# Activation tiles of a decoder kernel stored with padded rows

## Chip, cores and metric

The kernel runs on one core of a Trainium2 chip. The metric is the device time of one execution in microseconds; less is better.

## The reference

A trunk of two decoder layers over 256 tokens of width 1024, all in float32. Each layer:

```python
h = rms_norm(x, mix_norm[l])
z = h @ w_in[l]                       # 1024 -> 5632: u, q, k, v, two gates
y_a = s5_branch(u, ...)               # diagonal state-space scan, GELU, GLU
y_b = diff_attention(q, k, v, lam)    # 8 heads, two maps each
m = sigmoid(g_ssm) * (y_a @ w_proj_ssm[l]) + sigmoid(g_attn) * (y_b @ w_proj_attn[l])
x = x + m @ w_out[l]
h = rms_norm(x, ffn_norm[l])
f = swiglu(h, wg, wu, wd)             # layer 0: dense, 1024 -> 2816 -> 1024
f = moe_swiglu(h, ...)                # layer 1: the best 2 of 8 experts, each such a SwiGLU
x = x + f
```

A last RMSNorm ends it. Nearly all arithmetic is in products with weight matrices, about 390 MB of them in float32.

## The kernel before

**Products in three parts.** TensorE reads float32 operands as `fp32r`, which keeps fewer bits, so every operand is split into a high and a low part, and a product is made of three: high x high, low x high, high x low (`mm3`, L1938 to L1940). In the profile `psum<-w_hi,hsT_hi` names the moving operand first (w_hi, 512 columns wide) and the stationary one second (hsT_hi, 128 columns, loaded by an LDWEIGHTS of its own on PEld). The weight load for the next product runs while the present one streams.

**The weight stream.** All weights come as slots of 128 x 2048 floats. SP loads a slot into a ring `w_raw` (L660), ACT copies it to `w_hi` (rounding it, `act_split`, L599), DVE writes the rest to `w_lo` (`dve_split`, L605), PE uses the two. Segments 0 to 2 (mixer, dense layer, mixer) use a ring of three w_hi/w_lo places, the expert rounds five (two more, `w_hi_more` and `w_lo_more`). `split_of` gives the place of a slot; where the slot is to be stationary (`stationary`: gate and up slots of the dense layer outside ring position 1) it begins LEAD = 48 floats, 192 bytes, later.

**The activations.** They are needed with the model dimension on the partitions, so they are transposed on PE, copied out of PSUM by ACT (high part) and completed by DVE (low part). Four pairs of tiles matter:
- `hT_hi`, `hT_lo`: [128, 8, 256], the normed rows of all tokens in eight chunks. Stationary (128 of the 256 columns) for the 512-wide products of both mixers, written at L1009, L1140, L1463 and L1655; moving (all 256 columns) where the weights are stationary: the S5 input and the gate and up products of the dense layer. These are the 256-wide products.
- `hsT_hi`, `hsT_lo`: [128, 8, 128], the rows of one expert round, stationary for its gate and up products; written at L1195 and L1829.
- `eactT_hi`, `eactT_lo`: [128, 2, 4, 128], the activations of an expert round, stationary for its down products; written at L1216 and L1871.
- `actT`, `yS`, `yB`: the same for the dense layer and for the two mixer branches.

In all of them a chunk is a multiple of 512 bytes long, and so is each slot's. Before `w_lo` and before the region that begins with `a_q` the layout is rounded up so that they have the residue modulo 512 of `a_hT`; `w_hi` follows `w_raw` directly and has it too, since all ahead of it is a multiple of 512 long.

**The order.** Segment 0 (layer 0 mixer) lasts to about 254 us, segment 1 (dense layer) to 470, segment 2 (layer 1 mixer) to 685, then come eight expert rounds of 33 slots (`pe_round`; gate and up slots, with the down slots of earlier blocks between them). A round has 22 gate and up slots with 12 products each and 11 down slots with 12 each, 396 long products, and beside them 22 transposes of the activations and 8 of the next round's rows. In the dense layer the slots run g0, u0, g1, u1, d0, g2, u2, d1, and so on.

Of the kernel before, what the change touches and what calls it, by code (L numbers as in the profile page):

```python
# [8 lines left out]
F32 = mybir.dt.float32  # L9
F32R = mybir.dt.float32r  # L10
# [7 lines left out]
P = 128  # L18
SEQ, D, DEPTH = 256, 1024, 2
NT = SEQ // P  # L20
KD = D // P
# [23 lines left out]
SEG = 33  # L45
NRAW, NW, AHEAD = 4, 3, 2
LEAD = 48
RAW_POS = [i % 4 if i < 24 else (i - 24) % 3 for i in range(SEG)]
RAW_USES = [RAW_POS.count(p) for p in range(NRAW)]
GROUP_BLOCK = 512  # L50
# [148 lines left out]
def trunk(nc, t):  # L199
    ctx = ExitStack()  # L200
    with ctx:
        here = [(nc.sbuf_base + 63) // 64 * 64]

        def at(name, shape, dt, addr):
            return nc.alloc_sbuf_tensor_at(name, list(shape), dt, offset=addr)
# [7 lines left out]
        def sb(name, shape, dt=F32):  # L213
            a = here[0]
            here[0] += size(shape, dt)
            return at(name, shape, dt, a)

        def room(nbytes):
            a = here[0]
            here[0] += nbytes  # L220
            return a
# [3 lines left out]


        x = sb("x_tok", [P, NT, D])
        a_hT = room(16384)
        hTh = at("hT_hi", [P, KD, SEQ], F32R, a_hT)
        hTl = at("hT_lo", [P, KD, SEQ], F32R, a_hT + 8192)  # L230
        raw = sb("w_raw", [P, NRAW, SLOT])
        wh = sb("w_hi", [P, NW * SLOT + LEAD], F32R)
        here[0] += (a_hT - here[0]) % 512
        wl = sb("w_lo", [P, NW * SLOT + LEAD], F32R)
        ident = sb("ident", [P, P])
# [46 lines left out]


        here[0] += (a_hT - here[0]) % 512
        a_q, a_k, a_v = room(8192), room(8192), room(8192)
        a_u, a_yh, a_yl = room(4096), room(4096), room(4096)
        a_tab = room(32768)
        a_rr = room(16384)
# [44 lines left out]
        sg = at("silu_g", [P, 2 * SEQ], F32, a_q + 2048)  # L333
        aTh = at("actT_hi", [P, 2, 2, SEQ], F32R, a_u)
        aTl = at("actT_lo", [P, 2, 2, SEQ], F32R, a_yh)
        hsh = at("hsT_hi", [P, KD, P], F32R, a_k)
        hsl = at("hsT_lo", [P, KD, P], F32R, a_k + 4096)
        moe_act = at("eact_tok", [P, 512], F32, a_q)
        moe_sg = at("esilu_g", [P, 512], F32, a_q + 2048)
        bTh = at("eactT_hi", [P, 2, 4, P], F32R, a_hT)  # L340
        bTl = at("eactT_lo", [P, 2, 4, P], F32R, a_hT + 4096)
        rawx = at("w_raw_more", [P, 1, SLOT], F32, a_tab + 8192)
        whx = [at("w_hi_more0", [P, 1, SLOT], F32R, a_rr), at("w_hi_more1", [P, 1, SLOT], F32R, a_tab + 16384)]
        wlx = [at("w_lo_more0", [P, 1, SLOT], F32R, a_rr + 8192), at("w_lo_more1", [P, 1, SLOT], F32R, a_tab + 24576)]
# [98 lines left out]
        def bank(b):  # L443
            return PS[:, b, :]
# [107 lines left out]
        def raw_of(seg, i):  # L552
            p = (RAW_POS if seg < 3 else ROUND_POS)[i]
            return raw[:, p, :] if p < NRAW else rawx[:, 0, :]

        def stationary(seg, i):

            if seg == 1:
                return i % NW != 1 and FFN_SLOTS[i][0] != "d"
            return False  # L560

        def split_of(seg, i):

            p = i % NW if seg < 3 else ROUND_POS[i]
            if p < NW:
                a = (p + 2) % NW * SLOT + (LEAD if stationary(seg, i) else 0)
                return wh[:, a:a + SLOT], wl[:, a:a + SLOT]
            return whx[p - NW][:, 0, :], wlx[p - NW][:, 0, :]

        def landed(seg, i, r=None):  # L570

            if seg < 3:
                p = RAW_POS[i]
                return s_raw[p], 16 * (seg * RAW_USES[p] + RAW_POS[:i + 1].count(p))
            p = ROUND_POS[i]
# [70 lines left out]
        def _(sp):  # L646
            stream = t["stream"]

            def load(seg, i, src, r=None, ahead=False):

                if seg < 3:
                    before = seg * SEG + before_in(RAW_POS, i)
                    if before >= 0:
                        sp.wait_ge(s_lo, before + 1)
                elif r is PROLOGUE:

                    sp.wait_ge(s_lo, 3 * SEG + before_in(RAW_POS, i) + 1)
                else:
# [602 lines left out]
        def _(dve):  # L1261
            own = Own(dve, s_dve)
            V = nc.vector
# [187 lines left out]
            def lo_of(dst, src, hi, scale, n, last=True):  # L1451

                i = V.scalar_tensor_tensor(dst, src, scale, hi.bitcast(F32), ALU.mult, ALU.subtract)
                if last:
                    i.then_inc(s_trf[n % 2], 1)
# [96 lines left out]
            for l in range(DEPTH):  # L1552
# [9 lines left out]
                for s in range(SEG):  # L1562
# [3 lines left out]
                    if 0 <= s - 17 < HEADS:  # L1566
                        h = s - 17
                        n = TR_AT[l, "o", h]
# [23 lines left out]
                    if 0 <= s - 18 < HEADS:  # L1592
                        h = s - 18
                        n = TR_AT[l, "oT", h]
# [5 lines left out]
                    if 0 <= s - 16 < HEADS:  # L1600
                        h = s - 16
                        n = TR_AT[l, "wT", h]
# [47 lines left out]
                    if s in (28, 30):  # L1650
                        for g in (s - 28, s - 27):
                            n = TR_AT[l, "mT", g]
                            thi[0] += 1
                            dve.wait_ge(s_thi, thi[0])
                            lo_of(hTl[:, 2 * g:2 * g + 2, :].rearrange("p k n -> p (k n)"), bank(4 + n % 2),  # L1655
                                  hTh[:, 2 * g:2 * g + 2, :].rearrange("p k n -> p (k n)"), 0.5, n)
                    if s in (25, 26, 27, 29):
                        out_block(l, {25: PS0, 26: PS0 + 1, 27: PA0, 29: PA0 + 1}[s])
                    if s in (27, 29):
# [23 lines left out]
                n = 2 * l + 1  # L1683
# [90 lines left out]
            n = TR_AT[1, "logits", 0]  # L1774
# [23 lines left out]
            n = TR_AT[1, "places", 0]  # L1798
# [27 lines left out]
            V.tensor_tensor(G[:, :, :], oh1[:, :, :], oh2[:, :, :], ALU.add).then_inc(s_gates, 1)  # L1826

            def hs_lo(g):
                V.tensor_tensor(hsl[:, 4 * g:4 * g + 4, :].rearrange("p k n -> p (k n)"), bank(2 + g),  # L1829
                                hsh[:, 4 * g:4 * g + 4, :].rearrange("p k n -> p (k n)").bitcast(F32),  # L1830
                                ALU.subtract).then_inc(s_hsf, 1)

            dve_split(dve, 3, 1, PROLOGUE)
# [24 lines left out]
            def dve_round(r, first, last=False):  # L1858

                his = [0]  # L1860

                def hi_taken(name):

                    his[0] += 1
                    assert [w for w in ROUND_TR if w[:2] != "ST"][his[0] - 1] == name
                    dve.wait_ge(s_thi, r * NB + (THI0 + his[0]))
                    return TR0 + ROUND_TR.index(name)

                def act_lo(j):
                    t, n = hi_taken(f"act{j}"), block_width(j)  # L1870
                    V.tensor_tensor(bTl[:, j % 2, 0:n // P].rearrange("p k n -> p (k n)"), bank(4 + t % 2)[:, 0:n],  # L1871
                                    bTh[:, j % 2, 0:n // P].rearrange("p k n -> p (k n)").bitcast(F32),
                                    ALU.subtract).then_inc(s_trf[t % 2], 1)

                for i in range(SEG):
                    if last and i == 5:
                        dve.wait_ge(s_idx, 1)
                        dve.wait_ge(s_yw, r * 16)
                        V.tensor_copy(rowi[:, :, :], rowf[:, :, :]).then_inc(s_idx, 1)
                    if last and i in (10, 20):  # L1880
                        add_rows(i // 10 - 1)
                    if last and i == SEG - 1:
                        for q in range(NT):
                            n = TR0 + LAST_TR.index(f"ST{q}")
                            dve.wait_ge(s_tr, r * R_TR + (n + 1))
                            V.tensor_copy(ST[:, q * P:(q + 1) * P], bank(4 + n % 2)[:, 0:P]).then_inc(s_trf[n % 2], 1)
                    if i in (29, 31):
                        act_lo(4 + (i - 29) // 2)
                    if i in (30, 31) and not last:
                        dve.wait_ge(s_hsh, r * 2 + (2 + i - 29))  # L1890
                        hs_lo(i - 30)
                    if not last or i + RAHEAD < SEG:
                        round_split(dve_split, dve, i, r)
                    if last and i == 4:
                        own.do(V.tensor_copy(gcol[:, :], gateR[:, :, bass.ds(r, 1)].rearrange("p t o -> p (t o)")))
                    if i in (7, 13, 19, 25):
                        act_lo((i - 7) // 6)
                    if last and i == SEG // 2:
                        own.do(V.tensor_copy(pcol[:, :], placeR[:, :, bass.ds(r, 1)].rearrange("p t o -> p (t o)")))
                        select_last()  # L1900
                    if i in LAST_UP[:5] or i == 28:
                        j = LAST_UP.index(i) if i in LAST_UP else 5
                        n = block_width(j)
                        dve.wait_ge(s_sg, r * NB + (GU0 + j + 1))
                        if j == 5:
                            dve.wait_ge(s_tr, r * R_TR + (TR0 + ROUND_TR.index("act4") + 1))
                        ups = bank(3 + 4 * (j % 2)) if j < NB - 1 else bank(2 + 4 * (j % 2))[:, n:2 * n]
                        V.tensor_tensor(moe_act[:, 0:n], moe_sg[:, 0:n], ups[:, 0:n], ALU.mult).then_inc(s_act, 1)

                for c in range(2 if last else 0):  # L1910
                    dve.wait_ge(s_ysh, r * 2 + (2 + c + 1))
                    V.tensor_tensor(ysl[:, c * 512:(c + 1) * 512], bank(c), ysh[:, c * 512:(c + 1) * 512].bitcast(F32),
                                    ALU.subtract).then_inc(s_ysl, 1)
# [577 lines left out]
```

## Time and profile before

| | us |
|---|---|
| median of 3 runs | 1453.68 |
| lowest, highest | 1452.29, 1455.04 |
| span of the profiled execution | 1453.1 |
| PE busy | 1426.3 (98%) |
| PEld busy (weight loads) | 1202.9 (83%) |
| DVE busy | 1179.7 (81%) |
| ACT busy | 884.7 (61%) |

The profile is one execution, taken by the hardware profiler. Its engines: PE for matmuls, PEld for weight loads, which overlap PE, DVE, ACT, POOL, and SP, which here issues loads. A matmul's record is longer than its place in the stream: neighbouring records overlap. What a matmul costs in a run of equal ones is therefore read from the starts of neighbours in the timeline, not from its duration. Starts are printed to 0.01 us; over n spacings the error of the mean is 0.01 us / n.

### The profile page before, as it was taken

What the parts mean: (1) busy time and instruction counts of PE and PEld (TensorE: products, weight loads), DVE (VectorE), ACT (ScalarE), POOL (GpSimd) and SP (SyncE); (2) the same over time, 40 slices, a digit from 0 to 9 for tenths busy, and PEclk for the clock granted to TensorE, in tenths of its full rate; (3) what the DMA queues carried; (4) which work ended last, traced back from release to release, by engine and by line L of the source; (5) the groups of instructions that cost most, each with busy time, mean ns of one, the idle gap of its engine ahead of it and who ended that gap; (6) DMA issues with size and microseconds to landing.
All of it is one profiled execution on the core that took longest, in us unless ns stands there. A gap on an engine that the chain in (4) does not pass through costs nothing.

```text
span 1453.1 us, 22261 instructions
## 1 busy us (share of the span) xinstructions
PE 1426.3 (98%) x8381; PEld 1202.9 (83%) x8381; DVE 1179.7 (81%) x1181; ACT 884.7 (61%) x879; POOL 141.4 (10%) x195
## 2 busy tenths in 40 slices
PE   8999999999999999999999999999999999999997
PEld 6887888999998888887888888888888888888875
DVE  7998886676467697876988988889898898898896
ACT  5334754534344345644768768777777777777774
POOL 1910100000000000101960000000000000000100
PEclk9999999999999999999999999999999999999999
DMA  7443445776455442454999999999999999999993
GB/s 285 136 180 121 156 159 189 261 246 233 151 189 192 174 160 97 151 188 161 365 413 390 406 363 399 380 364 413 353 398 394 354 404 370 379 397 347 419 376 145
DMA packets 94247, 408.87 MB, mean 281 GB/s; under 512 B 28769, under 2 KB 43233, under 8 KB 47714
## 3 DMA queue, kind: packets, MB, share of 16 engines
q1 hardware_dynamic: 75984, 391.37, 69.9%
q10 hardware_dynamic: 17042, 12.36, 2.6%
q0 software_dynamic: 1152, 4.19, 0.7%
q8 instruction: 46, 0.75, 0.2%
q14 instruction: 23, 0.19, 0.0%
HBM read 390.98 MB, written 14.16 MB: 279 GB/s over the span
## 4 chain that ended last, share of the span: by engine, by line
PE 78%; DVE 11%; DMA 3%; SPq 3%; issue 2%; ACT 2%; POOL 1%; DVEq 0%; POOLq 0%; ACTq 0%
PE psum L1938 25%; PE psum L1940 24%; PE psum L1939 24%; DVE w_lo L605 4%; SPq L696 3%; PE psum L1954 2%; DMA w_raw<-in_stream 2%; DMA x_normed<-y_rows,row_number 1%; ACT w_hi L599 1%; ACT square_out L993 0%; PE psum L2284 0%; PE psum L2005 0%; DVE s_r L1511 0%; ACT prob L1129 0%; PE psum L1987 0%
## 5 line engine op out<-in xcount | busy, mean ns | idle before, releaser
L605 DVE TENSOR_TENSOR w_lo<-w_raw,w_hi 128x2048 fp32r<-128x2048 f32 x267 | 607.9, 2293 | 130.2 <-ACT w_hi L599 129.4
L599 ACT ACTIVATE w_hi<-w_raw 128x2048 fp32r<-128x2048 f32 x267 | 509.4, 1915 | 251.1 <-PE psum L1940 191.5
L1938 PE MATMUL psum<-w_hi,hsT_hi 128*128 128x512 f32 x448 | 176.0, 393 | 0.8 <-DVE hsT_lo L1829 0.8
L1940 PE MATMUL psum<-w_lo,hsT_hi 128*128 128x512 f32 x448 | 174.5, 390 | 0.0
L1939 PE MATMUL psum<-w_hi,hsT_lo 128*128 128x512 f32 x448 | 174.3, 389 | 0.0
L1938 PE MATMUL psum<-w_hi,hT_hi 128*128 128x512 f32 x376 | 152.7, 406 | 1.8 <-ACT gate_ssm L1075 1.4
L605 DVE TENSOR_TENSOR w_lo_more<-w_raw,w_hi_more 128x2048 fp32r<-128x2048 f32 x56 | 128.2, 2289 | 24.3 <-ACT w_hi_more L599 23.6
L1940 PE MATMUL psum<-w_lo,hT_hi 128*128 128x512 f32 x376 | 147.4, 392 | 0.0
L1939 PE MATMUL psum<-w_hi,hT_lo 128*128 128x512 f32 x376 | 147.1, 391 | 0.0
L599 ACT ACTIVATE w_hi_more<-w_raw 128x2048 fp32r<-128x2048 f32 x56 | 107.1, 1913 | 21.6 <-DMA w_raw<-in_stream 12.4
L1938 PE MATMUL psum<-hT_hi,w_hi 128*128 128x256 f32 x416 | 116.6, 280 | 0.2 <-DVE hT_lo L1463 0.2
L1940 PE MATMUL psum<-hT_lo,w_hi 128*128 128x256 f32 x416 | 116.5, 280 | 0.0
L1939 PE MATMUL psum<-hT_hi,w_lo 128*128 128x256 f32 x416 | 116.3, 280 | 0.0
L1938 PE MATMUL psum<-w_hi_more,hsT_hi 128*128 128x512 f32 x256 | 101.2, 395 | 0.0
L1940 PE MATMUL psum<-w_lo_more,hsT_hi 128*128 128x512 f32 x256 | 99.8, 390 | 0.0
L1939 PE MATMUL psum<-w_hi_more,hsT_lo 128*128 128x512 f32 x256 | 99.6, 389 | 0.0
L1938 PEld LDWEIGHTS psum<-w_hi,hsT_hi 128*128 128x128 f32 x448 | 84.1, 188 | 17.8 <-DVE w_lo L605 1.0
L1940 PEld LDWEIGHTS psum<-w_lo,hsT_hi 128*128 128x128 f32 x448 | 84.1, 188 | 17.8
L1939 PEld LDWEIGHTS psum<-w_hi,hsT_lo 128*128 128x128 f32 x448 | 84.2, 188 | 17.0
L605 DVE TENSOR_TENSOR w_lo_more<-w_raw_more,w_hi_more 128x2048 fp32r<-128x2048 f32 x40 | 91.4, 2285 | 1.2 <-ACT w_hi_more L599 1.2
L1938 PE MATMUL psum<-w_hi,eactT_hi 128*128 128x512 f32 x224 | 89.7, 401 | 1.6 <-DVE eactT_lo L1871 1.6
L1940 PE MATMUL psum<-w_lo,eactT_hi 128*128 128x512 f32 x224 | 87.4, 390 | 0.0
(429 smaller groups left out, 2651.2 us busy)
## 6 DMA issues: line engine op xcount, KB each, us to landing
w_raw<-in_stream SPq DMA_DIRECT2D x323, 1024.0 KB, 6.9
w_raw_more<-in_stream SPq DMA_DIRECT2D x40, 1024.0 KB, 7.7
h_rows<-one_row ACTq DMA_DIRECT2D x10, 512.0 KB, 6.6
round_rows<-h_rows SPq DMA_DIRECT2D x7, 512.0 KB, 7.0
y_rows<-y_slots ACTq DMA_DIRECT2D x7, 512.0 KB, 9.2
y_rows<-one_row ACTq DMA_DIRECT2D x4, 512.0 KB, 6.2
gain_row<-in_gain_rows SPq DMA_DIRECT2D x3, 512.0 KB
x_tok<-in_x SPq DMA_DIRECT2D x2, 512.0 KB, 6.2
```

The lines of the kernel that those rows point to most:

```text
L599: nc.scalar.activation(split_of(seg, i)[0], raw_of(seg, i), ACT.Copy).then_inc(s_hi, 1)
L605: nc.vector.tensor_tensor(l_, raw_of(seg, i), h.bitcast(F32), ALU.subtract).then_inc(s_lo, 1)
L696: sp.dma_start(zT[rows(g, q), j, :, :], quad(U4, g, j, q)).then_inc(s_zt, 16)
L1938: mm(out, lh, rh, start=start, stop=False)
L1939: mm(out, ll, rh, start=False, stop=False)
L1940: return mm(out, lh, rl, start=False, stop=stop)
L1954: i = nc.tensor.transpose(dst[:, k * P:(k + 1) * P], s, ident[:, :])
```

## The change

The rows of three pairs of tiles get a few floats of padding: 4 floats behind each 256 of hT, 16 behind each 128 of hsT, 20 behind each 128 of eactT. The rows of hT are then 1040 bytes apart, those of hsT 576, those of eactT 592. Every use reads and writes the unpadded part. Three DVE writers that treated several rows as one flat row now use them as rows. hsT grows by 1024 bytes, so what lies behind `a_k` moves by 1024 bytes; hT grows by 256 bytes in all, which moves `w_raw` and `w_hi` by 256, and the rounding ahead of `w_lo` takes these up. No instruction is added or taken away.

```diff
+HT_PAD, HS_PAD, BT_PAD = 4, 16, 20
...
-        a_hT = room(16384)
-        hTh = at("hT_hi", [P, KD, SEQ], F32R, a_hT)
-        hTl = at("hT_lo", [P, KD, SEQ], F32R, a_hT + 8192)
+        hT_bytes = 4 * KD * (SEQ + HT_PAD)
+        a_hT = room(2 * hT_bytes)
+        hTh = at("hT_hi", [P, KD, SEQ + HT_PAD], F32R, a_hT)[:, :, 0:SEQ]
+        hTl = at("hT_lo", [P, KD, SEQ + HT_PAD], F32R, a_hT + hT_bytes)[:, :, 0:SEQ]
         raw = sb("w_raw", [P, NRAW, SLOT])
         wh = sb("w_hi", [P, NW * SLOT + LEAD], F32R)
         here[0] += (a_hT - here[0]) % 512
...
-        a_q, a_k, a_v = room(8192), room(8192), room(8192)
+        hs_bytes = 4 * KD * (P + HS_PAD)
+        a_q, a_k, a_v = room(8192), room(2 * hs_bytes), room(8192)
...
-        hsh = at("hsT_hi", [P, KD, P], F32R, a_k)
-        hsl = at("hsT_lo", [P, KD, P], F32R, a_k + 4096)
+        hsh = at("hsT_hi", [P, KD, P + HS_PAD], F32R, a_k)[:, :, 0:P]
+        hsl = at("hsT_lo", [P, KD, P + HS_PAD], F32R, a_k + hs_bytes)[:, :, 0:P]
...
-        bTh = at("eactT_hi", [P, 2, 4, P], F32R, a_hT)
-        bTl = at("eactT_lo", [P, 2, 4, P], F32R, a_hT + 4096)
+        bT_bytes = 4 * 8 * (P + BT_PAD)
+        bTh = at("eactT_hi", [P, 2, 4, P + BT_PAD], F32R, a_hT)[:, :, :, 0:P]
+        bTl = at("eactT_lo", [P, 2, 4, P + BT_PAD], F32R, a_hT + bT_bytes)[:, :, :, 0:P]
...
-                V.tensor_tensor(hsl[:, 4 * g:4 * g + 4, :].rearrange("p k n -> p (k n)"), bank(2 + g),
-                                hsh[:, 4 * g:4 * g + 4, :].rearrange("p k n -> p (k n)").bitcast(F32),
+                V.tensor_tensor(hsl[:, 4 * g:4 * g + 4, :], bank(2 + g).rearrange("p (k n) -> p k n", n=P),
+                                hsh[:, 4 * g:4 * g + 4, :].bitcast(F32),
                                 ALU.subtract).then_inc(s_hsf, 1)
```

The low parts of hT at L1655 and of eactT at L1871 change in the same way as that of hsT.

## Rows read from the trace of the kernel before

**Rows 1.** The page: busy time, slices, loads, the chain that ended last.

```profile
PE 1426.3 (98%) x8381; PEld 1202.9 (83%) x8381; DVE 1179.7 (81%) x1181; ACT 884.7 (61%) x879; POOL 141.4 (10%) x195
PEclk9999999999999999999999999999999999999999
GB/s 285 136 180 121 156 159 189 261 246 233 151 189 192 174 160 97 151 188 161 365 413 390 406 363 399 380 364 413 353 398 394 354 404 370 379 397 347 419 376 145
PE 78%; DVE 11%; DMA 3%; SPq 3%; issue 2%; ACT 2%; POOL 1%; DVEq 0%; POOLq 0%; ACTq 0%
PE psum L1938 25%; PE psum L1940 24%; PE psum L1939 24%; DVE w_lo L605 4%; SPq L696 3%; PE psum L1954 2%; DMA w_raw<-in_stream 2%; DMA x_normed<-y_rows,row_number 1%; ACT w_hi L599 1%; ACT square_out L993 0%; PE psum L2284 0%; PE psum L2005 0%; DVE s_r L1511 0%; ACT prob L1129 0%; PE psum L1987 0%
```

**Rows 2.** Timeline of PE in a round: start, duration, line; first and last of 22.

```profile
800.03 0.39 PE L1940 MATMUL psum<-w_lo,hsT_hi 128*128 128x512 f32 x1
...
804.79 0.39 PE L1940 MATMUL psum<-w_lo,hsT_hi 128*128 128x512 f32 x1
```

**Rows 3.** The same in the dense layer: ends of slots u0, g1 with u1, g2 with u2.

```profile
260.45 0.28 PE L1938 MATMUL psum<-hT_hi,w_hi 128*128 128x256 f32 x1
...
266.21 0.28 PE L1938 MATMUL psum<-hT_hi,w_hi 128*128 128x256 f32 x1
...
277.09 0.40 PE L1938 MATMUL psum<-w_hi,actT_hi 128*128 128x512 f32 x1
...
282.55 0.28 PE L1938 MATMUL psum<-hT_hi,w_hi 128*128 128x256 f32 x1
...
293.86 0.40 PE L1938 MATMUL psum<-w_hi,actT_hi 128*128 128x512 f32 x1
```

**Rows 4.** Timeline: bf16 fillers; and their group, with the mean of one.

```profile
249.36 2.85 PE L1960 MATMUL psum<-maskb,identb 128*128 128x128 bf16 x48
...
L1960 PE MATMUL psum<-maskb,identb 128*128 128x128 bf16 x176 | 11.3, 219 | 0.0
```

**Rows 5.** Groups by line, one of three lines each: busy us, mean ns, idle before.

```profile
L1938 PE MATMUL psum<-w_hi,hsT_hi 128*128 128x512 f32 x448 | 176.0, 393 | 0.8 <-DVE hsT_lo L1829 0.8
L1938 PE MATMUL psum<-w_hi,hT_hi 128*128 128x512 f32 x376 | 152.7, 406 | 1.8 <-ACT gate_ssm L1075 1.4 <-DVE hT_lo L1463 0.4
L1938 PE MATMUL psum<-hT_hi,w_hi 128*128 128x256 f32 x416 | 116.6, 280 | 0.2 <-DVE hT_lo L1463 0.2
L1938 PE MATMUL psum<-w_hi_more,hsT_hi 128*128 128x512 f32 x256 | 101.2, 395 | 0.0
L1938 PE MATMUL psum<-w_hi,eactT_hi 128*128 128x512 f32 x224 | 89.7, 401 | 1.6 <-DVE eactT_lo L1871 1.6
L1938 PE MATMUL psum<-w_hi_more,eactT_hi 128*128 128x512 f32 x128 | 49.9, 390 | 0.0
```

**Rows 6.** The writers, by line: ns minimum/median/maximum, first and last start.

```profile
L1463 DVE TENSOR_TENSOR hT_lo<-psum,hT_hi x16: 672/682/692, 15.0 to 682.2; 128x512 fp32r<-128x512 f32 x16
L1829 DVE TENSOR_TENSOR hsT_lo<-psum,hsT_hi x16: 680/684/692, 691.7 to 1342.1; 128x512 fp32r<-128x512 f32 x16
L1009 ACT ACTIVATE hT_hi<-psum x16: 576/594/603, 12.7 to 681.6; 128x512 fp32r<-128x512 f32 x16
L1195 ACT ACTIVATE hsT_hi<-psum x16: 597/600/602, 690.0 to 1340.5; 128x512 fp32r<-128x512 f32 x16
```

**Rows 7.** Timeline of PE after an interruption in a round.

```profile
805.02 0.60 PE L1954 MATMUL psum<-ident,eact_tok 128*128 128x128 f32 x4
805.38 0.48 PE L1938 MATMUL psum<-w_hi,hsT_hi 128*128 128x512 f32 x1
805.69 0.40 PE L1939 MATMUL psum<-w_hi,hsT_lo 128*128 128x512 f32 x1
...
807.55 0.39 PE L1938 MATMUL psum<-w_hi,hsT_hi 128*128 128x512 f32 x1
```

**Rows 8.** Stretches: busy us (x instructions) of each engine, clock, DMA share, GB/s.

```profile
800.00:893.30 93.30, 93.30 (x427) 77.28 (x426) 82.25 (x48) 70.53 (x50) 0.00 (x0) 1.00 0.96 383
893.30:986.60 93.30, 93.30 (x427) 77.29 (x426) 82.03 (x48) 69.36 (x49) 0.00 (x0) 1.00 0.96 383
...
0.00:130.00 130.00, 123.38 (x1047) 101.67 (x1049) 118.82 (x210) 55.68 (x61) 47.93 (x58) 0.99 0.53 192
```

**Rows 9.** Waits from 700 to 1340 us: total us, times, longest.

```profile
DVE w_lo L605 <- ACT w_hi L599: 36.6, 63, 1.2
ACT w_hi L599 <- DMA w_raw<-in_stream: 33.2, 39, 2.0
```

**Rows 10.** The chain that ended last, its longest pieces: start, us, what.

```profile
59.79 1.57 DVE setup_tmp L1437
...
1345.42 9.52 DMA w_raw<-in_stream
...
1365.67 11.95 DMA x_normed<-y_rows,row_number
...
1391.31 10.05 DMA w_raw<-in_stream
```

**Rows 11.** Waits of SP's queue: total us, times, longest.

```profile
SPq L660 <- DVE w_lo L605: 876.0, 244, 21.8
```

More of the change, by code:

```diff
@@ L1654, in _ @@
                             dve.wait_ge(s_thi, thi[0])
-                            lo_of(hTl[:, 2 * g:2 * g + 2, :].rearrange("p k n -> p (k n)"), bank(4 + n % 2),
-                                  hTh[:, 2 * g:2 * g + 2, :].rearrange("p k n -> p (k n)"), 0.5, n)
+                            lo_of(hTl[:, 2 * g:2 * g + 2, :], bank(4 + n % 2).rearrange("p (k n) -> p k n", k=2),
+                                  hTh[:, 2 * g:2 * g + 2, :], 0.5, n)
                     if s in (25, 26, 27, 29):
@@ L1870, in act_lo @@
                     t, n = hi_taken(f"act{j}"), block_width(j)
-                    V.tensor_tensor(bTl[:, j % 2, 0:n // P].rearrange("p k n -> p (k n)"), bank(4 + t % 2)[:, 0:n],
-                                    bTh[:, j % 2, 0:n // P].rearrange("p k n -> p (k n)").bitcast(F32),
+                    V.tensor_tensor(bTl[:, j % 2, 0:n // P], bank(4 + t % 2)[:, 0:n].rearrange("p (k n) -> p k n", n=P),
+                                    bTh[:, j % 2, 0:n // P].bitcast(F32),
                                     ALU.subtract).then_inc(s_trf[t % 2], 1)
```

## The prediction

> **What bounds the kernel now.** I read the page first: PE is busy 98% of the span, its clock is 9 tenths or more in every slice, and the chain that ended last is PE for 78%, 73% of the span on the three product lines L1938 to L1940 [rows 1]. A busy PE is not yet a paced PE, because the matmul records overlap (390 ns each), so I went on to the starts of neighbouring matmuls. In the expert rounds (columns 512 wide, slots w_hi and w_lo moving, hsT stationary) 22 starts lie between 800.03 and 804.79 us with nothing else among them: 4.76 us / 21 = 226.7 ns from one to the next [rows 2]. That is the real price of a product.
>
> How much of it is streaming? Two shapes tell. The same products 256 wide, in the dense layer's second slot, take (266.21 - 260.45) / 48 = 120.0 ns [rows 3]. The 256 further columns cost 106.7 ns, so a column takes 0.417 ns (the 2.4 GHz level) and 512 columns 213.3 ns. So **13.3 ns** of every long product is no streaming, and 13.3 ns of the short ones too. The bf16 fillers, 128 wide, show how small that remainder can be: 47 spacings in 2.85 - 0.22 = 2.63 us are 56.0 ns each, 53.3 of it streaming, so 2.7 ns [rows 4].
>
> Is that remainder a matter of addresses? In the dense layer it is. Slots there are stationary, and `stationary()` starts them 192 bytes late (LEAD), except those in ring position 1. The second slot, without LEAD, gives 120.0 ns; the next two, with LEAD, give (277.09 - 266.21) / 96 = 113.3 ns; the pair before the second down slot, also with LEAD, gives (293.86 - 282.55) / 96 = 117.8 ns [rows 3]. Same shape, same engines, same clock: 192 bytes between the residues of the two operands are worth 2.2 ns or 6.7 ns. They are two steady values for one layout, so the state in which a run of products is entered counts as well. All other operands meet at equal residues, and all their long runs settle at 226 to 227 ns.
>
> The Trainium skill speaks against this change. SBUF — State Buffer, section Who interferes with whom, gives TensorE two independent read ports and says that PE never waits on anyone; by that the residues would change nothing. The 113.3 against 120.0 ns above is hard to reconcile with it. The sum below goes by the rows.
>
> **The change, part by part.**
>
> *Residues.* Rows of hT are now 1040 bytes, so its eight chunks begin at 0, 16, ... 112 modulo 512 (hT_lo 128 further); hsT steps by 64 through all of 0 to 448; eactT steps by 80, also eight values. Counts of products that read them as stationary, 512 wide: hsT 3 x (448 + 256) = 2112, eactT 3 x (224 + 128) = 1056, hT 3 x 376 = 1128 and 24 in the first slot [rows 5]. hT as moving operand: 3 x 416 = 1248.
>
> *The slot ring.* A side effect: the two hT tiles grow from 16384 to 16640 bytes, and w_hi lies behind w_raw with no alignment of its own, so the whole w_hi ring moves by 256 modulo 512. w_lo is aligned and stays. Two of three long products move w_hi, so yS, yB and actT, which nobody padded, meet it 256 bytes apart as well (552 long products); w_hi_more stays where it was.
>
> *Writers.* ACT and DVE now write rows with gaps. The trace has both forms. DVE takes 682 ns for 128x512 into four separate rows (L1463) and 684 ns into one flat row (L1829); ACT takes 594 against 600 ns (L1009, L1195) [rows 6]. Nothing, and none of them stands in the path for long. I take 0.
>
> *What a long product then costs* is not in this trace: no long product with unequal residues settles in it. Bounds from the nearest rows. Below: the best short product with unequal residues, 6.7 ns less. Still lower, the bf16 remainder of 2.7 ns in place of 13.3, 10.6 ns less. Above: the spacing before a run has settled. After the four transposes at 805.02 the starts from 805.69 to 807.55 are eight spacings of 232.5 ns, **5.8 ns more** than settled [rows 7]. For hsT and eactT, which go through eight residues, I take the middle of the two measured gains, (2.2 + 6.7) / 2 = 4.4 ns. For hT, whose shift stays small, I take 2.2 ns. For the 1248 short products, which have most of their offset already, 0 (bounds -4.5 and +2.2 ns from 117.8, so -5.6 to +2.7 us), and 0 for the 552 unpadded ones (-3.7 to +3.2 us).
>
> *What of it reaches the end.* The rounds run at a fixed period: 427 matmuls in each 93.3 us, PE never without work [rows 8]. From 700 to 1340 us no wait of PE is in the list, and those of ACT and DVE are covered [rows 9]. So a gain there counts in full, as long as the stream of weights follows. The last round is different: its chain has waits for w_raw loads (9.52 and 10.05 us), for the gather of y_rows (11.95 us) and for issue [rows 10]. And the first 130 us have the DVE, busy 118.8 of 130 us [rows 8], with chains of w_lo, setup and s_r pieces [rows 10]; the q, k, v and gate products of layer 0 lie there. I count seven rounds of eight, 7 x 396 = 2772 products (of 3168), and of the 1152 long hT products the 660 outside those 130 us.
>
> *The weights.* A round moves 383 GB/s with a DMA share of 0.96 to 0.97; the queue waits for w_lo to free a slot, and one slice reached 413, another 419 GB/s [rows 1, 8, 11]. At 413 a round could not be shorter than 93.3 x 383 / 413 = 86.5 us. A gain of 4.4 ns x 396 = 1.7 us leaves 91.6 us, at 390 GB/s: it fits. ACT already waits 33.2 us in these rounds for loads [rows 9], so a much larger gain would be cut short here, while the slots hold.
>
> **The sum:** 2772 x 4.4 ns = 12.2 us, 660 x 2.2 ns = 1.5 us, together 13.7 us. The profiled span is 1453.1 us, which is 0.6 us under the median of the three times, 1453.68, and inside their range; I take the 13.7 us off the median: **1440 us**.
>
> **Rivals.**
>
> *A. The settled state is lost* (slower). After an interruption the spacings wander (between 220 and 240 ns by the starts) and then stop at 226.7, and stay there for as long as each product is followed by an equal one [rows 7]. With padded rows no product is: the residue changes with every k, and w_hi and w_lo now differ by 256. If settling needs a constant pattern, every long product keeps the unsettled mean, 5.8 ns more. Price: (2772 + 660) x 5.8 = 19.9 us, and the 552 unpadded add up to 3.2: 1474 to 1477 us; half of it, when only some residues are bad, 1464 us. For it speaks that unsettled spacings are nearly all above the settled one. Against it, that three unequal-residue pairs of slots are faster, and steady. It decides from the point where the mean of long products passes 226.7 ns.
>
> *B. The remainder goes nearly whole* (much faster). Each long product falls towards 216.0 ns: (2772 + 660) x 10.6 = 36.4 us, 1417 us. A round would be 89.1 us, at 401 GB/s; the loads would just follow. For it, only the bf16 row, whose weights are smaller.
> In a sentence of its own: TensorE: Matmul & The Clock Gate, section Back-to-back issue gap, gives an isolated gap of N / 2.4 + 2.5 ns, that is an estimate of about 216 ns for 512 columns; by the skill that would be the price already today, and the trace's 226.7 does not agree.
>
> *C. Nothing for long products.* The relief belongs to short ones, where the load of the next weights (188 ns a record) fills the whole product, and a long one has 100 ns left after it. Or the independent ports of the skill hold after all, and the differences in rows 3 have another cause. Time 1453 us, plus or minus 2.
>
> *D. A smaller gain*: only 2.2 ns on everything, 3432 x 2.2 = 7.6 us, 1446 us.
>
> **How the numbers follow.** Forecast (4.4 ns, own range 1432 to 1443) 0.33; D (1444 to 1450) 0.14; B (below 1432) 0.10; C 0.15; A 0.28, of it 0.18 below 1468 and 0.10 above. About 0.2% (2.9 us) is what a measurement can tell from no change. Faster: 0.33 + 0.14 + 0.10 = 0.57; same 0.15; slower 0.28. The range for 8 in 10 leaves out the outer part of B and of A: 1420 to 1468 us. It crosses zero because no row shows a long product with unequal residues; without A it would be 1432 to 1450.
>
> **What would show it.** In the profile after: counts of instructions as before; spacing of long hsT products near 222 ns, and rounds of about 91.6 us, for the forecast; 232 ns and over 95 us for A; 226.7 ns for C. The ratio of w_raw slots (w_hi shifted) to w_raw_more slots (w_hi_more not shifted) shows what the ring's 256 bytes do. DVE and ACT writers should stay at 684 and 600 ns. The prediction is wrong if the spacing falls and the rounds stay at 93.3 us (then the loads were the bound), or if the clock or another engine has changed.

## The result, and the profile after

The change makes the kernel slower: 1470.93 us median (1467.13 to 1471.58, 4 runs) against 1452.99 us (1451.63 to 1455.04, 4 runs) for the kernel before in the same comparison. The ratio is 1.012, 95% interval 1.0105 to 1.0134. The forecast was 1440 us: the sign was wrong, and the time lies 2.9 us above the range.

The page of the profile after, its busy line, clock line and chain. All lines of the code stand 4 lower than before, so the products are L1942 to L1944:

```profile
span 1469.0 us, 22261 instructions
PE 1442.8 (98%) x8381; PEld 1204.2 (82%) x8381; DVE 1180.3 (80%) x1181; ACT 882.9 (60%) x879; POOL 141.5 (10%) x195
PEclk9999999999999999999999999999999999999999
PE 87%; DVE 8%; ACT 1%; SPq 1%; issue 1%; DMA 1%; POOL 0%; POOLq 0%; DVEq 0%; ACTq 0%
PE psum L1942 27%; PE psum L1943 27%; PE psum L1944 27%; PE psum L1958 3%; DVE w_lo L609 3%; SPq L700 1%; DMA w_raw<-in_stream 1%; PE psum L2009 1%; ACT square_out L997 0%; PE psum L2054 0%; PE psum L2288 0%; ACT w_hi L603 0%; ACT prob L1133 0%; PE psum L2070 0%; PE psum L1991 0%
```

The same instructions (8381 matmuls, as in [rows 1]), the same clock, the other engines busy for the same time within 2 us. PE is busy 16.5 us longer, and the span is 15.9 us longer than the 1453.1 before. The chain is PE for 87% instead of 78% [rows 1]: PE covers what it had waited for.

Where it went is told by the windows (busy us and number of instructions of PE, PEld, DVE, ACT and POOL, then clock, DMA share, GB/s):

```profile
800.00:895.10 95.10, 95.10 (x427) 77.45 (x426) 81.65 (x48) 70.56 (x50) 0.00 (x0) 1.00 0.96 375
895.10:990.20 95.10, 95.10 (x428) 77.45 (x427) 82.13 (x49) 70.02 (x50) 0.00 (x0) 1.00 0.95 375
0.00:130.00 130.00, 122.22 (x1037) 99.67 (x1039) 118.38 (x210) 55.66 (x61) 47.94 (x58) 1.00 0.55 192
```

A round's 427 matmuls take 95.10 us where they took 93.3 [rows 8]. The stream of weights now moves 375 GB/s instead of 383. It is slower because PE is, not the reverse: ACT waits less for loads in the rounds than before, 25.6 us over 640 us of rounds (715 to 1355 us) against the 33.2 of [rows 9]. The 1.8 us are 4.5 ns for each of the 396 long products. The spacing itself is read from starts in the timeline of PE:

```profile
800.02 0.40 PE L1942 MATMUL psum<-w_hi_more,hsT_hi 128*128 128x512 f32 x1
...
804.88 0.39 PE L1942 MATMUL psum<-w_hi_more,hsT_hi 128*128 128x512 f32 x1
...
886.77 0.39 PE L1942 MATMUL psum<-w_hi,hsT_hi 128*128 128x512 f32 x1
...
906.00 0.40 PE L1944 MATMUL psum<-w_lo,hsT_hi 128*128 128x512 f32 x1
```

The first two are 21 spacings: 4.86 / 21 = 231.4 ns; the last two are 83, over seven slots, five of them with w_hi and two with w_hi_more: 19.23 / 83 = **231.7 ns**, against 226.7 [rows 2]. Slots with w_hi_more, whose place in memory did not move by 256, and slots with w_hi, which did, cost the same: taken apart over the whole trace, the mean is 231.7 ns for either. Two more pairs from the same timeline, the unpadded yB (its w_hi is 256 bytes off) and the short products of g2 and u2:

```profile
208.51 0.39 PE L1942 MATMUL psum<-w_hi,yB_hi 128*128 128x512 f32 x1
...
219.17 0.39 PE L1944 MATMUL psum<-w_lo,yB_hi 128*128 128x512 f32 x1
...
283.91 0.28 PE L1942 MATMUL psum<-hT_hi,w_hi 128*128 128x256 f32 x1
...
295.30 0.40 PE L1942 MATMUL psum<-w_hi,actT_hi 128*128 128x512 f32 x1
```

10.66 / 47 = 226.8 ns for yB, unchanged. 11.39 / 96 = 118.6 ns for the short ones, 0.8 more than the 117.8 of [rows 3]. The writers, with rows that have gaps (ns minimum, median, maximum; first and last start):

```profile
L1199 ACT ACTIVATE hsT_hi<-psum x16: 597/599/600, 694.0 to 1356.8; 128x512 fp32r<-128x512 f32 x16
L1833 DVE TENSOR_TENSOR hsT_lo<-psum,hsT_hi x16: 678/682/692, 695.7 to 1358.4; 128x512 fp32r<-128x512 f32 x16
```

599 and 682 ns against 600 and 684 [rows 6]: nothing.

Last, marks by which the two traces can be laid side by side: fillers at the ends of the first mixer, of the dense layer and of the second mixer, the transposes of eact_tok, those of round_rows. Four lines of before (the first fillers of before stand in [rows 4]), then the five of after:

```profile
450.98 0.40 PE L1960 MATMUL psum<-maskb,identb 128*128 128x128 bf16 x4
676.88 2.17 PE L1960 MATMUL psum<-maskb,identb 128*128 128x128 bf16 x36
L1954 PE MATMUL psum<-ident,eact_tok x176: 270/272/273, 711.7 to 1434.9; 128*128 128x128 f32 x176
L2284 PE MATMUL psum<-ident,round_rows x56: 270/272/273, 776.7 to 1340.2; 128*128 128x128 f32 x56
```

```profile
250.26 2.85 PE L1964 MATMUL psum<-maskb,identb 128*128 128x128 bf16 x48
453.17 0.40 PE L1964 MATMUL psum<-maskb,identb 128*128 128x128 bf16 x4
680.83 2.17 PE L1964 MATMUL psum<-maskb,identb 128*128 128x128 bf16 x36
L1958 PE MATMUL psum<-ident,eact_tok x176: 270/273/273, 716.1 to 1450.7; 128*128 128x128 f32 x176
L2288 PE MATMUL psum<-ident,round_rows x56: 271/273/273, 782.2 to 1356.5; 128*128 128x128 f32 x56
```

The first fillers (249.36 before) are 0.9 us late, the first eact_tok 4.4, the first round_rows 5.5, the last round_rows 16.3, the last eact_tok 15.8, the end 15.9. So the loss grows by 10.8 us over the six rounds between 777 and 1340 us, and the last round does not grow at all. The marks ahead of the rounds are less sure. The one at 451 us stands at 449.2 in a run in which nothing ahead of the rounds was padded (e2 below), so 2 us there are no price. The second mixer by itself, from the second fillers to the third, is steadier: 225.9 us before, 227.7 after, 225.9 in e2. Its 576 long hT products cost 1.8 us, 3.1 ns each.

### The profile page after: what moved, and what is told of

Its sections match the earlier page's. It is cut to its first block, busy times and chain, and to the rows that moved or that the text cites. A ratio compares the mean times of both kernels' runs of the same rounds, so it can differ in the third digit from the quotient of the medians.

```text
span 1469.0 us, 22261 instructions
## 1 busy us (share of the span) xinstructions
PE 1442.8 (98%) x8381; PEld 1204.2 (82%) x8381; DVE 1180.3 (80%) x1181; ACT 882.9 (60%) x879; POOL 141.5 (10%) x195
## 4 chain that ended last, share of the span: by engine, by line
PE 87%; DVE 8%; ACT 1%; SPq 1%; issue 1%; DMA 1%; POOL 0%; POOLq 0%; DVEq 0%; ACTq 0%
PE psum L1942 27%; PE psum L1943 27%; PE psum L1944 27%; PE psum L1958 3%; DVE w_lo L609 3%; SPq L700 1%; DMA w_raw<-in_stream 1%; PE psum L2009 1%; ACT square_out L997 0%; PE psum L2054 0%; PE psum L2288 0%; ACT w_hi L603 0%; ACT prob L1133 0%; PE psum L2070 0%; PE psum L1991 0%
## 5 line engine op out<-in xcount | busy, mean ns | idle before, releaser
L1942 PE MATMUL psum<-w_hi,hsT_hi 128*128 128x512 f32 x448 | 178.1, 397 | 0.8 <-DVE hsT_lo L1833 0.8
L1944 PE MATMUL psum<-w_lo,hsT_hi 128*128 128x512 f32 x448 | 176.3, 394 | 0.0
L1942 PE MATMUL psum<-w_hi,hT_hi 128*128 128x512 f32 x376 | 153.1, 407 | 2.0 <-ACT gate_ssm L1079 1.4
L1944 PE MATMUL psum<-w_lo,hT_hi 128*128 128x512 f32 x376 | 148.5, 395 | 0.0
L1942 PE MATMUL psum<-hT_hi,w_hi 128*128 128x256 f32 x416 | 117.3, 282 | 0.7 <-DVE w_lo L609 0.5
L1944 PE MATMUL psum<-hT_lo,w_hi 128*128 128x256 f32 x416 | 116.8, 281 | 0.0
L1942 PE MATMUL psum<-w_hi_more,hsT_hi 128*128 128x512 f32 x256 | 102.3, 400 | 0.0
L1944 PE MATMUL psum<-w_lo_more,hsT_hi 128*128 128x512 f32 x256 | 100.8, 394 | 0.0
L1942 PEld LDWEIGHTS psum<-w_hi,hsT_hi 128*128 128x128 f32 x448 | 84.4, 188 | 19.7 <-DVE w_lo L609 0.9
L1944 PEld LDWEIGHTS psum<-w_lo,hsT_hi 128*128 128x128 f32 x448 | 84.2, 188 | 19.7
L1942 PE MATMUL psum<-w_hi,eactT_hi 128*128 128x512 f32 x224 | 90.2, 402 | 0.0
L1943 PE MATMUL psum<-w_hi,eactT_lo 128*128 128x512 f32 x224 | 88.6, 395 | 0.0
```

The source lines that it names most:

```text
L1942: mm(out, lh, rh, start=start, stop=False)
L1943: mm(out, ll, rh, start=False, stop=False)
L1944: return mm(out, lh, rl, start=False, stop=stop)
```

## The experiments

Every kernel below is the kernel before with the edit shown (and with the three DVE writers in their form by rows); the ratio is to the kernel before on the same chip. "Distance" is the start of the stationary operand less that of the moving one, modulo 512 bytes. Before, it is 0 for all long products; for the short ones it is 192, and 0 in ring position 1 of the dense layer and in the S5 input. The spacings are means over settled runs of equal products, in which nothing else stands.

### e1_ring_64: only the moving operand's place

```diff
+        room(64)
         wh = sb("w_hi", [P, NW * SLOT + LEAD], F32R)
```

No tile is padded; the three w_hi places lie 64 bytes later, w_hi_more stays.

> Only the w_hi ring moves, by 64 bytes; all stationary tiles stay unpadded and w_lo and w_hi_more stay where they were. Theory T (a run of products settles when the stationary chunks keep one residue; where the moving operand begins does not matter): w_hi products stay at 226.7 ns, the time within 0.2% of before. Rival R (the residue between moving and stationary operand sets the spacing, and 256 bytes happened to be as good as 0): products with w_hi moving leave 226.7 ns, those with w_hi_more do not; at 5 ns on two thirds of some 3400 products on the path that is 11 us, about 1464 us.

Measured: 1468.94 us, ratio 1.0101 (1.0082 to 1.0119). A w_hi slot and the w_hi_more slot behind it, in the timeline:

```profile
889.62 0.39 PE L1941 MATMUL psum<-w_lo,hsT_hi 128*128 128x512 f32 x1
...
894.52 0.39 PE L1941 MATMUL psum<-w_lo,hsT_hi 128*128 128x512 f32 x1
...
895.20 0.39 PE L1941 MATMUL psum<-w_lo_more,hsT_hi 128*128 128x512 f32 x1
...
899.96 0.39 PE L1941 MATMUL psum<-w_lo_more,hsT_hi 128*128 128x512 f32 x1
```

4.90 / 21 = 233.3 ns, and three products later 4.76 / 21 = 226.7 ns. The same stationary tile, the same clock, the same shape: 64 bytes in the start of one operand make 6.6 ns. Theory T is refuted and rival R holds, with a higher price than the 5 ns that it was given. It holds for all stationary tiles: hsT 233.4, hT 232.5, actT 233.4, yB 233.3, yS 233.6. The Trainium skill, SBUF — State Buffer, section Who interferes with whom, lets PE's two ports work independently and never wait; this pair of slots disagrees with what one would conclude from it, that the starts of operands are indifferent. Only the two w_hi products of a chunk stand 64 bytes away, yet the mean over all three is 233.3. Which of the three steps is the long one is no fixed matter: for hsT the steps behind the two w_hi products are 234.8 and 234.3 ns and the one behind the w_lo product (its distance is 0) 231.5; for actT they are 230.9, 233.4 and 236.2.

### e2, e3, e4: one pair of tiles at a time

```diff
# e2_hsT_only
+        hsh = at("hsT_hi", [P, KD, 144], F32R, a_k + 0)[:, :, 0:P]
# e3_eactT_only
+        bTh = at("eactT_hi", [P, 2, 4, 148], F32R, a_hT + 0)[:, :, :, 0:P]
# e4_hT_only
+        hTh = at("hT_hi", [P, KD, 260], F32R, a_hT + 0)[:, :, 0:SEQ]
```

The low tiles change in the same way, and what lies behind a tile moves by a multiple of 512 bytes. e4 also brings the 256 bytes of the w_hi ring. The spacings in the expectations are those of the profile after; what is tested is the time of each part and whether the other tiles stay.

> Only hsT is padded (16 floats). hsT products 231.6 ns instead of 226.7, eactT and hT products stay at 226.7 ns. 2112 products, about 1848 of them in the seven rounds that PE sets: 4.9 ns x 1848 = 9 us, about 1462 us. If the padded tiles act only together, no change.

> Only eactT is padded (20 floats). eactT products 232.1 ns, the others stay: 924 products in seven rounds x 5.4 ns = 5 us, about 1458 us.

> Only hT is padded (4 floats), and with it the w_hi ring moves by 256 bytes as in the change. Long hT products 231.5 ns, short ones 118.7 instead of 118.1, hsT and eactT stay at 226.7 ns: 660 x 4.8 + 1000 x 0.6 = 4 us, about 1457 us. If it was the ring's 256 bytes that cost, the hsT products with w_hi slow down here too and those with w_hi_more do not, and the time comes near 1465 us.

| | median us | ratio (95%) | more us | spacing of the padded tile |
|---|---|---|---|---|
| hsT only | 1462.33 | 1.0062 (1.0043 to 1.0081) | 9.0 | 231.5 |
| eactT only | 1458.72 | 1.0032 (1.0019 to 1.0046) | 4.7 | 232.1 |
| hT only | 1455.39 | 1.0021 (1.0009 to 1.0032) | 3.0 | 231.6 |

The extra microseconds are (ratio - 1) x 1453. All other tiles stay at 226.7 ns in each of the three, in e4 with w_hi 256 bytes away as well, so the ring's 256 bytes are free. The parts add up to 16.7 us, against 17.4 for the whole change (0.012 x 1453): no interplay is needed. Each part is also its count times its spacing: hsT 2112 x 7/8 x 4.8 ns = 8.9 us; eactT 1056 x 7/8 x 5.4 ns = 5.0 us; hT 660 x 4.9 ns = 3.2 us. The last of the three agrees by luck. The 660 is the prediction's count, and the trace of before has 816 long hT products behind 130 us; 576 of them, the second mixer, cost 3.1 ns each (above), not 4.9. A likely reason, not tested: before the change many of them stand in stretches of twelve between interruptions, and those take 228 to 231 ns already.

### e5, e6: a constant distance, no padding

Is the loss due to the change of residue from product to product, as rival A had it, or to the distance as such? Here whole tiles begin later, so the distance is the same in every product of a run.

```diff
# e5_const_a: hT 64, hsT 128, eactT 192 bytes later
+        hTh = at("hT_hi", [P, KD, 256], F32R, a_hT + 64)[:, :, 0:SEQ]
+        hsh = at("hsT_hi", [P, KD, 128], F32R, a_k + 128)[:, :, 0:P]
+        bTh = at("eactT_hi", [P, 2, 4, 128], F32R, a_hT + 192)[:, :, :, 0:P]
# e6_const_b: hT 192, hsT 64, eactT 128
```

The low tiles move with the high ones here and in e9 to e11.

> No padding. Whole tiles begin later by a constant: hT by 64 bytes, hsT by 128, eactT by 192 (high and low parts alike). Theory E (a long product is cheap only where stationary and moving operand begin at equal residues modulo 256): all three leave 226.7 ns, hT for about 233, hsT and eactT for something between 227 and 236; the time rises by 10 to 20 us. Rival K (what matters is that the distance between the operands stays the same from product to product): all three settle, at 226.7 ns or at a value of their own below it, and the time stays at 1453 us or falls.

> As the run before with other constants: hT 192, hsT 64, eactT 128 bytes; in the dense layer hT then meets the gate and up slots at distance 0 instead of 192, except the second slot. E: long products 228 to 236 ns, each offset the same in either tile, and short gate and up products at 120.0 ns (the second slot's 117.8 or 113.3). K: long products settled at 226.7 ns or lower.

Measured: e5 1470.95 us, ratio 1.0119 (1.0102 to 1.0136); e6 1470.87 us, 1.0124 (1.0107 to 1.0141). In the timeline of e5, 46 spacings with hT at distance 64:

```profile
235.06 0.39 PE L1939 MATMUL psum<-w_hi,hT_lo 128*128 128x512 f32 x1
...
245.79 0.40 PE L1940 MATMUL psum<-w_lo,hT_hi 128*128 128x512 f32 x1
```

In that of e6, the same 46 with hT at distance 192, the 96 short products of g2 and u2, now at distance 0, and 83 spacings with hsT at 64:

```profile
234.95 0.39 PE L1939 MATMUL psum<-w_hi,hT_lo 128*128 128x512 f32 x1
...
245.49 0.40 PE L1940 MATMUL psum<-w_lo,hT_hi 128*128 128x512 f32 x1
...
283.85 0.28 PE L1938 MATMUL psum<-hT_hi,w_hi 128*128 128x256 f32 x1
...
295.36 0.39 PE L1938 MATMUL psum<-w_hi,actT_hi 128*128 128x512 f32 x1
...
884.22 0.40 PE L1938 MATMUL psum<-w_hi,hsT_hi 128*128 128x512 f32 x1
...
903.58 0.40 PE L1940 MATMUL psum<-w_lo,hsT_hi 128*128 128x512 f32 x1
```

10.73 / 46 = 233.3 ns at distance 64, 10.54 / 46 = 229.1 ns at 192, 19.36 / 83 = 233.3 ns at 64 again. Constant distances settle too, only at another value: theory E holds, rival K does not. What settles is the mean. Single steps go in a fixed pattern, 235.8 and 230.8 ns in turn for hsT at 64, where at distance 0 every step is 226 or 227. And the short products went from 117.8 to 11.51 / 96 = 119.9 ns by being brought to distance 0. **Distance 0 is the best of these for long products and the worst for short ones.** That is the pair of facts on which the prediction broke.

### e8 to e11: the table of distances

A kernel e7, with hT at 256, hsT at 32 and eactT at 16 bytes, gave no result. The distances 16 and 32 were measured in e9 and e11 in its place, and 256 with hsT.

```diff
# e8_steps: eactT steps by 768 bytes (distances 0 and 256 in turn), hsT by 544 (32-byte steps)
+        bTh = at("eactT_hi", [P, 2, 4, 192], F32R, a_hT + 0)[:, :, :, 0:P]
+        hsh = at("hsT_hi", [P, KD, 136], F32R, a_k + 0)[:, :, 0:P]
# e9_const_d: hsT 32, eactT 96 bytes later, short products at 64
+LEAD = 16
+        hsh = at("hsT_hi", [P, KD, 128], F32R, a_k + 32)[:, :, 0:P]
+        bTh = at("eactT_hi", [P, 2, 4, 128], F32R, a_hT + 96)[:, :, :, 0:P]
# e10_const_e: hsT 160, eactT 224, LEAD = 56 (short ones at 224)
# e11_const_f: hsT 256, eactT 16, LEAD = 32 (short ones at 128)
```

> Rows padded: eactT by 64 floats (chunks begin at 0 and 256 in turn), hsT by 8 floats (32 bytes a step). E: eactT stays at 226.7 ns although its residue modulo 512 changes with every chunk; hsT rises as in the change, to 229 to 232 ns, 4 to 9 us. If any change of the residue is what costs, eactT rises to 232 ns too.

> Constants again, no padding: hsT 32 bytes, eactT 96; hT stays, but the gate and up slots of the dense layer begin 64 bytes late instead of 192 (LEAD = 16). Theory E: 0 and 256 are the only good distances, so hsT lies between 227 and 233 ns and eactT between 230 and 234. A rival says that only multiples of 64 bytes matter: then hsT stays at 226.7. The short products at distance 64: one of the two settled values 113.3 or 117.8 ns; if 113.3 everywhere, the dense layer gains 1008 x 4.5 = 4.5 us.

> hsT 160 bytes, eactT 224, LEAD = 56 (224 bytes). E with a smooth dependence on the distance: hsT near 231 ns, eactT near 228. Short products at distance 224 between 113.3 and 120 ns.

> hsT 256 bytes, eactT 16, LEAD = 32 (128 bytes). E: hsT stays at 226.7 ns although it lies 256 bytes off; eactT near 227 to 230. Short products at distance 128: 119 to 120 ns, as hT at that distance in an earlier run.

| | median us | ratio (95%) |
|---|---|---|
| e8_steps | 1461.91 | 1.0063 (1.0047 to 1.008) |
| e9_const_d | 1471.34 | 1.0118 (1.0088 to 1.0147) |
| e10_const_e | 1469.71 | 1.0106 (1.0073 to 1.0139) |
| e11_const_f | 1456.30 | 1.0026 (1.0013 to 1.0039) |

Timeline of e8: 22 spacings of eactT; then 83 of hsT.

```profile
1157.09 0.39 PE L1939 MATMUL psum<-w_hi,eactT_lo 128*128 128x512 f32 x1
...
1162.08 0.39 PE L1940 MATMUL psum<-w_lo_more,eactT_hi 128*128 128x512 f32 x1
```

```profile
878.67 0.39 PE L1938 MATMUL psum<-w_hi,hsT_hi 128*128 128x512 f32 x1
...
897.87 0.39 PE L1940 MATMUL psum<-w_lo,hsT_hi 128*128 128x512 f32 x1
```

4.99 / 22 = 226.8 ns for eactT: chunks at changing places, 0 and 256, cost nothing there. In the whole trace they are not quite free: of the 81 stretches of eactT 24 take 229.8 to 230.2 ns, a value that no stretch of before has. That is some 0.8 us (an estimate, a quarter of 924 products at 3.1 ns). 19.20 / 83 = 231.3 ns for hsT: steps of 32 bytes cost as much as steps of 64. Timeline of e9, hsT at 32; of e11, hsT at 256 and eactT at 16, in two stretches:

```profile
882.88 0.40 PE L1938 MATMUL psum<-w_hi,hsT_hi 128*128 128x512 f32 x1
...
902.25 0.39 PE L1940 MATMUL psum<-w_lo,hsT_hi 128*128 128x512 f32 x1
```

```profile
879.12 0.40 PE L1938 MATMUL psum<-w_hi,hsT_hi 128*128 128x512 f32 x1
...
897.95 0.40 PE L1940 MATMUL psum<-w_lo,hsT_hi 128*128 128x512 f32 x1
...
780.38 0.39 PE L1939 MATMUL psum<-w_hi,eactT_lo 128*128 128x512 f32 x1
...
785.37 0.39 PE L1940 MATMUL psum<-w_lo_more,eactT_hi 128*128 128x512 f32 x1
...
1247.78 0.40 PE L1939 MATMUL psum<-w_hi,eactT_lo 128*128 128x512 f32 x1
...
1252.91 0.40 PE L1940 MATMUL psum<-w_lo_more,eactT_hi 128*128 128x512 f32 x1
```

19.37 / 83 = 233.4 ns at 32, 18.83 / 83 = 226.9 at 256. At 16 bytes the first stretch takes 4.99 / 22 = 226.8 ns and the second, of the same products in a later round, 5.13 / 22 = 233.2; 62 of the 81 stretches of eactT are at 226.7. The expectation of e10 failed: it had 231 ns at 160 and 228 at 224, and both took 233.3 or a little more. In e9 hsT left 226.7 at 32 bytes, so not only multiples of 64 cost. Of the two values for the short products nearly all took the dearer, 117.8. All constant distances together (ns from one product to the next; two values: both occur as settled states; a range: stretches of the trace differ, and most lie in it):

| distance | 0 | 16 | 32 | 64 | 96 | 128 | 160 | 192 | 224 | 256 |
|---|---|---|---|---|---|---|---|---|---|---|
| long, 512 wide | 226.7 | 226.7 / 233.3 | 233.4 | 233.3 | 234.3 | 231.7 to 233.3 | 233.3 to 233.8 | 228.9 to 229.5 | 233.3 | 226.7 to 226.9 |
| short, 256 wide | 120.0 | | | 113.3 / 117.8 | | 118.7 / 120.0 | | 113.3 / 117.8 | 116.7 / 117.8 | |

So 256 is as good as 0, and 16 bytes can be enough for the whole price. That the other distances repeat after 256 bytes too (320 like 64, say) was not run by itself. For long products nothing tried is better than what the kernel before has. For short ones 224 bytes (116.7) might be a little better than the 192 it has; by 1.1 ns on the some 1000 short products outside ring position 1 that would be 1 us, under what can be measured here, and it was not run by itself.

### e12_low_only: which step grows

```diff
+        hTl = at("hT_lo", [P, KD, 256], F32R, a_hT + 8384)[:, :, 0:SEQ]
+        hsl = at("hsT_lo", [P, KD, 128], F32R, a_k + 4160)[:, :, 0:P]
+        bTl = at("eactT_lo", [P, 2, 4, 128], F32R, a_hT + 4224)[:, :, :, 0:P]
```

Only the low tiles lie later (hT_lo 192, hsT_lo 64, eactT_lo 128), so one product in three has a distance.

> Only the low stationary tiles move, by a constant: hsT_lo 64 bytes, eactT_lo 128, hT_lo 192; high tiles at 0. Three products per chunk: (w_hi moving, high stationary), (w_hi, low), (w_lo, high); the weights of each are loaded while the one before it streams. Theory C (the load of the next weights collides with the stream that runs meanwhile): the step that grows most is the one behind the product during which the low tile is loaded, (w_hi, hsT_hi), to about 234 ns, the other two less, to 229 to 232. Rival W (a product waits for its own weights, so the low one starts late, or is slow itself): the step behind (w_hi, hsT_lo) grows most. Mean of hsT products between 229 and 233 ns, time 1460 to 1470 us; if one disturbed load in three were all that counts, the mean would be 226.7 + 6.6 / 3 = 228.9 ns and the time 1457 us.

Measured: 1466.09 us, ratio 1.009 (1.006 to 1.0119). Timeline:

```profile
802.66 0.39 PE L1938 MATMUL psum<-w_hi,hsT_hi 128*128 128x512 f32 x1
802.89 0.40 PE L1939 MATMUL psum<-w_hi,hsT_lo 128*128 128x512 f32 x1
803.13 0.39 PE L1940 MATMUL psum<-w_lo,hsT_hi 128*128 128x512 f32 x1
803.35 0.39 PE L1938 MATMUL psum<-w_hi,hsT_hi 128*128 128x512 f32 x1
```

For hsT the step behind L1939, the product whose own two operands differ, is the longest: 235.8 ns in the mean over the seven-slot stretches; behind L1940 it is 228.3, behind L1938 229.2. Rival W said this, and the 234 ns behind L1938 that theory C expected did not come. Yet it does not decide between them, since single steps do not show whose operands cost:

- In the same run the steps of eactT stand in another order, 234.4 behind L1938, 232.7 behind L1939 and 230.9 behind L1940.
- Where all three products have the same distance the steps differ as much: 230.9, 231.7 and 237.4 for hsT at 160 (e10).
- In e2 the steps in chunks whose distance is 0 are 235.7, 228.3 and 229.1, where a product that is charged its own distance would take 226.7.

What e12 does show is the mean. It is 231.1 ns, all three steps are above 226.7, and a mean of the table would be (2 x 226.7 + 233.3) / 3 = 228.9. So in a mixed pattern a product is not simply charged its own distance. Whether the load of the next weights takes part stays open.

## Why the prediction was wrong, step by step

**The bound: right.** PE at a fixed period sets the time. The spacing changed, and rounds went from 93.3 to 95.10 us while PE stayed busy throughout. The terms that were set to zero were zero: DVE and ACT writers (682 and 599 ns), the unpadded tiles (226.8), the 256 bytes of the ring (231.7 with w_hi_more and with w_hi; 226.7 for hsT with either in e4). The products in the first 130 us indeed count for little: +0.9 us in all by the fillers at 250 us. The count behind them was wrong, though: 816 long hT products start after 130 us, not 660. It hardly moved the sum (156 x 2.2 ns = 0.3 us). Seven rounds of eight indeed: between the last round_rows and the last eact_tok lie 94.7 us before and 94.2 after, though its products are slower too, and 94.9 and 94.8 in e9 and e10, where they are slower still. What covers them is read from the chain: the 11.95 us for y_rows and the two loads of 9.52 and 10.05 us stand in the chain of before [rows 10], the chain after has no such pieces, and its page has DMA at 1% instead of 3%. That link was read from the two chains and not tested by a run.

**The step that failed** is the one that begins "For hsT and eactT, which go through eight residues, I take the middle of the two measured gains". The gains (2.2 and 6.7 ns, [rows 3]) were measured on 256-wide products with w_hi as the stationary operand, and were carried over to 512-wide ones. The measured value is +4.9 ns, not -4.4. Same bytes, same engine, opposite sign: e6 shows both in one kernel, 119.9 ns for short products at distance 0 and 229 to 233 ns for long ones away from it. The reasoning before it, that 13.3 ns of either shape are "no streaming" and so one and the same remainder, could not have come out otherwise: a price per column that is taken from the difference of two widths leaves the same remainder in both. Where both stand 64 bytes apart the same sum gives (233.3 - 117.8) / 256 = 0.451 ns a column and 2.3 ns left, so it is no term that the two shapes share. And 226.7 and 120.0 are the best of the long and the worst of the short ones. Even for short products 4.4 ns was too much: of the 21 slots with LEAD in the trace of before 19 take 117.8 ns (2.2 less), and only g1 and u1 take 113.3. The step for hT (2.2 ns less) failed in the same way (231.6, 4.9 more), and the short products took 0.8 ns more where 0 stood, within its bounds.

**Rival A had the sign and nearly the size.** Both of its signs came, a spacing near 232 ns (231.7) and rounds of over 95 us (95.10). It took 5.8 ns from the unsettled spacings [rows 7], 19.9 us; measured are 4.9 ns and 17.4 us. Its count of 3432 products x 4.9 ns gives 16.8 us. Its mechanism is right in part at most. Constant distances settle in the mean, at 233.3 ns (e5, e6), and changing ones at 226.8 when they are multiples of 256 (e8): most of the loss is the distance itself. That the mixed patterns of e1 and e12 cost more than the mean of the table, and that a quarter of the stretches in e8 take 3 ns more, leaves room for something of A. For the whole change the table gives, for the four distances of hsT modulo 256, (226.7 + 233.3 + 233.3 + 229.2) / 4 = 230.6 ns; measured 231.7.

**Rival C's evidence was there and got too little weight.** It said that the relief belongs to short products. It expected 226.7 for long ones, which is wrong too, and its 100 ns left after the load of the weights has no row: a record of 188 ns in a spacing of 226.7 leaves 39. But the doubt behind it, that a price for one shape says nothing on another, was the one that mattered.

**The range was cut below A's own sum.** A was worked out at 1474 to 1477 us and had 0.28, more than the 0.2 that the range could leave out together with B's 0.10; part of A was put below 1468 on a guess that only some residues are bad (of the constant distances tried, 0 and 256 alone are free, and 16 in part of the stretches). Keeping A's sum inside would have held the time. With one unmeasured quantity, multiplied by 3432 products, both signs of it had a row in the trace: -6.7 and +5.8 ns.

**What stays open.** What inside PE or its reads makes the distance count. Whether the load of the next weights takes part. Why 16 bytes have two states for long products, and 64 and 192 for short ones. Why 192 is milder than its neighbours, and yet e1, whose w_hi products stand at -64, that is 192 modulo 256, takes the full 6.6 ns. And whether it is a distance at all: in each run one operand moved against the others, never both by the same amount.

## What to carry to other kernels

A kernel paced by back-to-back matmuls has their place in SBUF as a parameter: here the starts of moving and stationary operand apart by a multiple of 256 bytes gave 226.7 ns for 512-wide fp32r products, almost any other distance 229 to 234, and the padded rows, 4.9 ns dearer, are 1.2% of a kernel when they touch some 3400 of its 8400 matmuls. For 256-wide products the other distances were better or equal (120.0 ns at distance 0, 113.3 to 117.8 at 64 and 192, 118.7 or 120.0 at 128), so a layout found for one shape has to be measured again for the next. Before a whole change, one run that pads one tile gives the price per product for that shape, from the starts of neighbours, and for hsT and eactT the count times that price was the result to within a microsecond (e2, e3). The price of a constant shift (2.2 to 7.6 ns) is not that of padding.

## What the hardware showed that was not expected

- 64 bytes in the start of the moving operand alone, between two neighbouring slots with the same stationary tile: 233.3 against 226.7 ns (e1).
- 256 bytes are as good as 0: long products at 256 stay at 226.7 to 226.9 ns (e11), and so do most that alternate between 0 and 256 (e8).
- Opposite reaction of two widths: from distance 0 to 64, long products +6.6 ns, short ones -2.2 or -6.7 ns (e6, e9).
- Two settled values for one layout: 113.3 and 117.8 ns for short products at 64 and at 192, 226.7 and 233.3 ns for long ones at 16 bytes (e11).
- A settled mean can hide a pattern: at a constant distance of 64 bytes the single steps are 235.8 and 230.8 ns in turn (e6), at 160 they are 230.9, 231.7 and 237.4 (e10); at distance 0 all are 226 or 227.
